# Softmax attention in a long single-core kernel: two fp32r score products on all 128 rows from stored high and low parts, and a differential unit that takes its second map whole before its first

## What is computed

```python
def diff_attention(q1, q2, k1, k2, v, lam):
    s1 = jnp.einsum('bqhd,bkhd->bhqk', q1, k1).astype(jnp.float32) * ATTN_SCALE
    s2 = jnp.einsum('bqhd,bkhd->bhqk', q2, k2).astype(jnp.float32) * ATTN_SCALE
    w = jax.nn.softmax(s1, axis=-1) - lam * jax.nn.softmax(s2, axis=-1)
    return jnp.einsum('bhqk,bkhe->bqhe', w, v.astype(jnp.float32))
...
def sink_attention(qg, k, v, sink, valid):
    s = jnp.einsum('bqhgd,bkhd->bhgqk', qg, k).astype(jnp.float32) * ATTN_SCALE
    ...
    p = jax.nn.softmax(jnp.concatenate([s, sink_col], axis=-1), axis=-1)[..., :-1]
    return jnp.einsum('bhgqk,bkhd->bqhgd', p, v.astype(jnp.float32))
```

## Time and profile before

| what | value |
|---|---|
| median of 3 runs | 3462.72 us (3462.21 to 3463.39) |
| span of the profiled execution | 3460.9 us, 1.8 below that median |
| mean granted TensorE clock | 0.962 |
| phase p0 beside the side job | 220 to 455 us |
| phase att: loads and context units | 459 to 504 us |
| phase att: 32 pairs | 504.8 to about 885 us |

### The profile page before, as it was taken

How to read it: one execution, slowest core, us unless ns; L and a number is a source line. 1 busy time by engine, 2 the same in 40 slices (tenths; PEclk the granted TensorE clock), 3 DMA queues, 4 the chain that set the end, 5 groups by cost and what they waited for, 6 DMA issues and landing times. The chain is left out here.

```text
span 3460.9 us, 51322 instructions
## 1 busy us (share of the span) xinstructions
PE 3176.7 (92%) x20902; PEld 2807.3 (81%) x20902; DVE 1711.3 (49%) x2697; ACT 1221.1 (35%) x2257; POOL 298.4 (9%) x357
## 2 busy tenths in 40 slices
PE   7999979999798999897999997979988999999988
PEld 4999967777587999775888976767856999999877
DVE  3459736666472211265526216746645445454343
ACT  4313235666562343124534114544423111111232
POOL 1000011100010000111211100002200000000010
PEclk9999999999899999998999998989999999999999
DMA  5556560000443221234211335110022111112332
GB/s 185 162 179 226 182 215 20 25 13 13 159 156 95 79 78 60 99 119 143 102 47 41 93 99 138 38 7 2 3 86 79 49 48 42 48 46 73 99 133 92
DMA packets 199262, 309.34 MB, mean 89 GB/s; under 512 B 43016, under 2 KB 133896, under 8 KB 197020
## 3 DMA queue, kind: packets, MB, share of 16 engines
q1 hardware_dynamic: 178448, 232.54, 21.1%
q0 software_dynamic: 20624, 74.13, 6.6%
HBM read 229.80 MB, written 76.81 MB: 89 GB/s over the span
## 5 line engine op out<-in xcount | busy, mean ns | idle before, releaser
L115 PE MATMUL p_pb<-p_w_hi,h_hi 128*128 128x416 f32 (+2 forms) x1168 | 408.2, 349 | 12.2 <-DVE p_w_lo L110 6.8
L116 PE MATMUL p_pb<-p_w_lo,h_hi 128*128 128x416 f32 (+2 forms) x1168 | 403.9, 346 | 0.0
L117 PE MATMUL p_pb<-p_w_hi,h_lo 128*128 128x416 f32 (+2 forms) x1168 | 403.8, 346 | 0.0
L115 PE MATMUL fu_pf<-h_hi,fu_w_hi 128*128 128x344 f32 (+1 forms) x1056 | 339.5, 322 | 8.7 <-DVE fu_pf L3747 8.7
L116 PE MATMUL fu_pf<-h_lo,fu_w_hi 128*128 128x344 f32 (+1 forms) x1056 | 340.5, 322 | 0.0
L117 PE MATMUL fu_pf<-h_hi,fu_w_lo 128*128 128x344 f32 (+1 forms) x1056 | 338.9, 321 | 0.0
L115 PEld LDWEIGHTS p_pb<-p_w_hi,h_hi 128*128 128x128 f32 x1168 | 221.0, 189 | 13.9 <-issue 12.6
L116 PEld LDWEIGHTS p_pb<-p_w_lo,h_hi 128*128 128x128 f32 x1168 | 220.7, 189 | 1.5
L117 PEld LDWEIGHTS p_pb<-p_w_hi,h_lo 128*128 128x128 f32 x1168 | 220.4, 189 | 1.3
L115 PEld LDWEIGHTS fu_pf<-h_hi,fu_w_hi 128*128 128x128 f32 x1056 | 199.9, 189 | 9.1 <-DVE fu_pf L3747 9.1
L117 PEld LDWEIGHTS fu_pf<-h_hi,fu_w_lo 128*128 128x128 f32 x1056 | 199.9, 189 | 0.0
(11 more groups left out here) (555 smaller groups left out, 6948.9 us busy)
## 6 DMA issues: line engine op xcount, KB each, us to landing
fu_raw<-in_ffn_up SPq DMA_DIRECT2D x88, 256.0 KB, 3.1
fd_raw<-in_ffn_down SPq DMA_DIRECT2D x44, 512.0 KB, 3.6
p_slab<-in_adaln_w SPq DMA_DIRECT2D x64, 256.0 KB, 3.3
la_qkv<-p SPq DMA_DIRECT2D x16, 1024.0 KB, 5.0
p<-p_o SPq DMA_DIRECT2D x60, 208.0 KB, 2.1
s_raw<-in_w_in POOLq DMA_DIRECT2D x48, 256.0 KB, 3.7
rT<-p_stage SPq DMA_DIRECT2D x10, 896.0 KB, 5.2
p_raw<-in_ab_w_in POOLq DMA_DIRECT2D x10, 832.0 KB, 7.2
```

The costliest lines, as they stand in the source:

```text
L115: pe.matmul(out, left[0], right[0], start=start, stop=False)
L116: pe.matmul(out, left[0], right[1], start=False, stop=False)
L117: return pe.matmul(out, left[1], right[0], start=False, stop=stop)
```

## The change

- The side job now stores two parts of each transposed block: a high part rounded to fp32r (ScalarE) and the rest (VectorE, `low_out`). The two A key heads are no longer doubled: 13 blocks, not 14. `rotated` is one buffer, not two, and the squares go to `tmp`.
- `rT` has the two parts as its first axis. Keys are loaded with their high part on partitions 0 to 63 and their low part on 64 to 127; a tile's queries are loaded with each part on both halves, into two buffers `Q` that are refilled tile by tile. Each load goes to 64 partitions, and SP issues them all.
- A score is now two fp32r products on all 128 rows (`whole`): the query's high part, then its low part, against the stacked keys.
- A `da` unit takes map 1 whole in part 0 and map 0 whole in part 1, and VectorE and ScalarE follow in that order. The waits change with it.

```diff
-                    sp.dma_start(rT[:, :, i * P:i * P + P].rearrange("c p t -> p c t"), stage[:, :, :]).then_inc(stage_out, 16)
+                    for part in range(2):
+                        sp.dma_start(rT[part, :, :, i * P:i * P + P].rearrange("c p t -> p c t"), stage[part][:, :, :].bitcast(F32)).then_inc(stage_out, 16)
...
-                    act.activation(stage[:, :, :], pt[:, 0:14, :], ACT.Copy).then_inc(evac, 1)
+                    act.activation(stage[0][:, :, :], pt[:, 0:QK_HEADS // 2, :], ACT.Copy).then_inc(staged, 1)
...
                         if i:
-                            dve.wait_ge(rotated, i)
+                            dve.wait_ge(turned, i)
...
+                def low_out(i):
+                    dve.wait_ge(staged, i + 1)
+                    lo_part(dve, stage[1][:, :, :], pt[:, 0:QK_HEADS // 2, :], stage[0][:, :, :]).then_inc(evac, 1)
...
-                sp.dma_start(KB[:, :, SEQ:], rT[KB_AT:KB_AT + 4, :, SEQ:].rearrange("c p t -> p c t")).then_inc(kb_ctx_in, 16)
...
+                def load_keys(keys, at, chunks, tokens, came):
+                    for part, half in enumerate(halves):
+                        sp.dma_start(keys[half, :, at:at + tokens.stop - tokens.start].bitcast(F32),
+                                     rT[part, chunks, :, tokens].rearrange("c (e d) t -> d (c e) t", d=HD)).then_inc(came, 16)
+
+                def load_queries(tile, first, chunk, came):
+                    for part in range(2):
+                        for half in halves:
+                            sp.dma_start(Q[ring[tile] % 2][half, first:first + 8, part, :].bitcast(F32),
+                                         rT[part, chunk:chunk + 4, :, P * tile:P * tile + P].rearrange("c (e d) t -> d (c e) t", d=HD)
+                                         ).then_inc(came[ring[tile] % 2], 16)
...
                 for tile in tiles_in_order:
+                    if ring[tile] + 2 < len(tiles_in_order):
+                        after = tiles_in_order[ring[tile] + 2]
+                        sp.wait_ge(scores, exps_before[last_of[tile] + 1])
+                        load_queries(after, A_HEADS, QB, qb_in)
+                        load_queries(after, 0, QA, qa_in)
...
-                pool.wait_ge(q1_in, 16)
+                pool.wait_ge(va_in, 16)
...
-                        for m in range(2):
-                            act.wait_ge(negmax, n + m + 1)
+                        for i, m in enumerate((1, 0)):
+                            act.wait_ge(negmax, n + i + 1)
...
-                        pe.wait_ge(expd, n - 1 if near_before else n)
+                        pe.wait_ge(expd, n - 2 if near_before and kind == "da" else n)
...
+                    def whole(out, head, keys, stop):
+                        queries = Q[ring[token_tile(u)] % 2]
+                        pe.matmul(out, queries[:, head, 0, :], keys, start=True, stop=False)
+                        return pe.matmul(out, queries[:, head, 1, :], keys, start=False, stop=stop)
+
                     if kind == "da":
-                        for c0, c1 in ((0, 512),) if part == 0 else ((512, 1024), (1024, ALLT)):
-                            for m, half in enumerate(halves):
-                                mm = pe.matmul(pS[m][:, c0:c1], qT[half, QB + j, q], KB[half, j, c0:c1], start=True, stop=True)
-                                if c1 == ALLT:
-                                    mm.then_inc(scores, 1)
+                        m = 1 - part
+                        for c0, c1 in ((0, 512), (512, 1024), (1024, ALLT)):
+                            mm = whole(pS[m][:, c0:c1], A_HEADS + 2 * j + m, KB[:, 2 * j + m, c0:c1], True)
+                        mm.then_inc(scores, 1)
...
                     if u < NU:
+                        n_tile = ring[token_tile(u)]
+                        pe.wait_ge((qb_in if units[u][0] in ("da", "dac") else qa_in)[n_tile % 2], 64 * (n_tile // 2 + 1))
```

More of the change, by code:

```diff
@@ L664, in project_even @@
         tmp = ph.sb("tmp", [P, QK_HEADS, HD])
-        rot = [ph.sb(f"rotated{s}", [P, 28, HD]) for s in range(2)]
+        rot = ph.sb("rotated", [P, QK_HEADS, HD])
         ss = ph.sb("ss", [P, QK_HEADS])
         rt = ph.sb("rt", [P, QK_HEADS])
-        stage = ph.sb("stage", [P, 14, P])
+        stage = ph.pair("stage", [P, QK_HEADS // 2, P])
         slab = [ph.sb(f"slab{s}", [P, MOD_BLK]) for s in range(2)]
@@ L852, in side @@
                         dve.wait_ge(spread, i + 1)
[L853 to L857, removed]
+                        dve.tensor_tensor(rot[:, :, :], rot[:, :, :], tmp[:, :, :], ALU.add).then_inc(rotated, 1)
+                        if i:
+                            low_out(i - 1)
+                    yield turn_at(n_all - 1) + 7
+                    low_out(n_all - 1)
+                def low_out(i):
+                    dve.wait_ge(staged, i + 1)
+                    lo_part(dve, stage[1][:, :, :], pt[:, 0:QK_HEADS // 2, :], stage[0][:, :, :]).then_inc(evac, 1)
                 def terms(i, k):
@@ L1268, in score @@
                         which = 0 if t == 0 else 2 if t == NT - 1 else 1
-                        left = [qT[half, QA + j, q] for half in halves]
-                        right = [KA[half, kv, :] for half in halves]
                         if part == 0:
                             for e in range(2):
-                                pe.matmul(pS[0][:, KEYS * e:KEYS * e + W3], left[e], right[e][:, near], start=True, stop=False)
-                            for e in range(2):
+                                whole(pS[0][:, KEYS * e:KEYS * e + W3], 2 * j + e, KA[:, kv, near], False)
                                 edges = pS[0][:, KEYS * e:KEYS * e + W3].rearrange("p (b k) -> p b k", b=3)[:, 0:3:2, :]
-                                mm = pe.matmul(edges, unit_r[:, :], mask[:, which, :, :], start=False, stop=True)
-                            mm.then_inc(banked, 1)
+                                pe.matmul(edges, unit_r[:, :], mask[:, which, :, :], start=False, stop=True)
                             return
-                        pe.matmul(pS[0][:, W3:512], left[0], right[0][:, far:far + P], start=True, stop=True)
-                        pe.matmul(pS[0][:, KEYS + W3:2 * KEYS], left[1], right[1][:, far:far + CTX], start=True, stop=True)
-                        pe.wait_ge(banked, sinks_before[u] - 3)
-                        pe.matmul(pS[0][:, 512:KEYS], left[0], right[0][:, far + P:far + CTX], start=True, stop=True).then_inc(scores, 2)
+                        whole(pS[0][:, W3:512], 2 * j, KA[:, kv, far:far + P], True)
+                        whole(pS[0][:, 512:KEYS], 2 * j, KA[:, kv, far + P:far + CTX], True)
+                        whole(pS[0][:, KEYS + W3:2 * KEYS], 2 * j + 1, KA[:, kv, far:far + CTX], True).then_inc(scores, 2)
                     elif part == 0:
```

88 lines of the change are left out of this document (41 added, 47 removed).

## The result

The changed kernel takes 3522.07 us (median of 4 runs, 3520.63 to 3524.55), the kernel before on the same chip 3463.05. The ratio is 1.0169, 95% interval [1.0155, 1.0184]: 59 us slower, where 40 were forecast. The time lies one microsecond inside the forecast's range of 3479 to 3523, and outside the 3489 to 3517 that had 0.6. Both costs of the forecast are there, and both are larger.

What follows compares the result with a forecast made beforehand. TensorE was taken as busy nearly all the time, with DMA to watch at the attention start. +22.6 + 1.5 + 17.6 - 1.1 = +40.6 on 3460.9 gave 3501.5, as median 3503 us; range 3479 to 3523.

Steps and rivals of the forecast that it cites:

- Both costs of the forecast: Late start of the attention phase, +22.6 us, and longer pairs, +17.6 us; forecast 3489 to 3517 us with chance 0.6.
- +22.6 us: Attention phase start: tile 0's B queries land at 527.4, where the first `da` unit started at 504.78.
- 11.8 MB at 210: Attention phase start: half-partition loads through tile 0's B queries, at 210 GB/s, take 56.2 us.
- 1.5 for the clock: First pair: TensorE starts at a lower clock after 20 us of standing, 1.5 us added.
- +17.6 us: The 32 pairs: 24 longer by 0.50 us and 8 with a press longer by 0.70.
- the last piece stays 4.26: Press pairs: transposes and value products with VectorE's row sum stay 4.26 us, so these pairs grow 0.70.
- a standing of 1.6 us should not lower the clock: Pairs: TensorE's wait of 1.60 us before the `wa` scores leaves its granted clock at 1.00.
- -1.1 us: p0 phase: 13 transposes instead of 14 in each of ten tiles save 1.1 us.
- Full-rate loads: Rival: attention phase loads run at full rate, start costs +2, rest as forecast; about 3481 us, chance 0.1.
- Gaps kept: Rival: TensorE's gaps between row shapes stay in the pairs, +37 there; +60 in all, 3523 us, chance 0.12.
- Both costs about half: Rival: queries land early through queue gaps and the pairs' wait is partly covered; 3475 to 3485 us, chance 0.1.
- The rival in which the window unit finds the second exponential done: Pairs: `wa` unit pays only its own work, 10.55 us a pair, -35 us, kernel near 3450; chance 0.05.

Runs made afterwards that it cites:

- experiment 1: Changed kernel, but ScalarE takes map 0's exponential first and the window scores wait for it alone: 3476.76 us, ratio 1.0044 to the kernel before.
- experiment 4: Kernel before the change, each key and query load cut into two of 64 partitions on the same queue: 3464.34 us, ratio 1.0003.
- experiment 6: Changed kernel with 128-partition loads from 192 DRAM rows per head: 3494.88 us; the faster one also takes map 0's exponential first: 3454.35 us.
- experiment 5: Kernel of experiment 1 with upper-half loads issued by POOL: 3487.68 us; with tile 0's queries ahead of A keys and values: 3479.94; both: 3482.26.

## Why the prediction was right, and where its sizes were off

**The direction and both mechanisms hold.** The wait on the second exponential was put at 1.60 us a pair; it measured 1.55, and taking it away (experiment 1) gave back 41.5 us over 31 intervals. The late start was put down to 64-partition loads at 210 GB/s and to doubled bytes; the windows show 205, experiment 4 shows that the rate is the partitions', and experiment 6 took 29 of the 33 us away.

**"+22.6 us" for the start: mis-sized, 32.7 measured from the start of the phase, and 4.0 more in the first pair.** The sum "11.8 MB at 210", values at 390 and nothing else comes to 15.5 MB at 236 GB/s on average. By the time the B queries are there, 16.3 MB have moved at 211:

```profile
457.50:534.60 77.10, 29.30 (x196) 27.27 (x194) 18.54 (x45) 21.00 (x78) 4.90 (x12) 0.70 1.10 211
458.00:473.00 15.00, 4.25 (x33) 4.05 (x32) 0.17 (x1) 0.00 (x0) 3.32 (x9) 0.73 1.10 187
519.00:523.00 4.00, 0.00 (x0) 0.00 (x0) 0.00 (x0) 0.00 (x0) 0.00 (x0) 0.50 1.04 375
525.00:529.00 4.00, 0.00 (x0) 0.00 (x0) 0.00 (x0) 0.00 (x0) 0.00 (x0) 0.50 1.20 167
```

As an estimate from these windows and the packets of the trace, three terms make most of the 10 us. Loads that the sum doesn't have were in flight beside the last queries, 0.4 MB of POOL's modulation sums and 0.3 MB of the next queries: 3.5 us. The B values' packets of 2,048 bytes took some 130 to 190 ns each while 64-partition loads were still in flight and 88 ns once they were alone (375 GB/s from 519 to 523), so these 2.6 MB took 9.2 us where 390 GB/s gives 6.7: 2.5. The first 15 us ran at 187 instead of 210: 1.6. The rest is 205 to 208 instead of 210 for the other halves, and less for short pieces, 167 from 525 to 529. No run takes these terms apart. The first pair, with 1.5 for the clock, also had the wait of 2.4 us for tile 0's A queries, which the sum did not have: it asked only when the B half lands.

**"+17.6 us" for the pairs: 24.7 measured.** Normal pairs were forecast 0.08 short (2 us in all), and three of them, ahead of the last three press pairs, are 12.6 (1 more). The press pairs carry the rest. Six of the eight are 13.79, 0.91 more than the 12.88 of before (one stood at 13.31), where "the last piece stays 4.26" gave 0.70: VectorE's maximum starts 0.37 us behind the transposes where it was 0.19, and the piece is 4.5. Two are 15.76 and 15.35. One of them, in windows:

```profile
750.00:752.00 2.00, 2.00 (x17) 1.61 (x17) 1.30 (x1) 0.60 (x1) 0.00 (x0) 1.00 0.04 10
752.00:754.00 2.00, 1.95 (x16) 1.67 (x14) 1.85 (x4) 1.30 (x4) 1.33 (x2) 1.00 0.00 0
754.00:756.00 2.00, 0.77 (x3) 0.67 (x4) 1.97 (x3) 0.73 (x3) 1.66 (x1) 1.00 0.00 0
756.00:758.00 2.00, 2.00 (x9) 1.89 (x8) 1.36 (x3) 0.10 (x1) 0.56 (x1) 0.51 0.39 156
```

TensorE was busy for 0.77 of 2 us, and then had a granted clock of 0.51, the lower of its two levels (1.2 GHz). The sentence "a standing of 1.6 us should not lower the clock" holds for the normal pairs, which stay at 1.00, and fails for these two. They are 1.6 and 2.0 us longer than the other six; in the longer one about 0.4 is a longer wait at the press, for with 128-partition loads (experiment 6, without the new order) the same pair is 14.19 and stays at 1.00. The other is 15.38 there, with the same dip, so the half-rate loads are not its cause. The second exponential is not needed either: experiment 6's faster kernel has one such pair, 14.49. All these dips follow a stand of 1.3 us at a press, but pair 20 of the changed kernel stands for 1.4 and keeps 1.00; what tells them apart is not shown.

**"-1.1 us" for p0: about -0.7.** The phase began at 454.2 to 458.4 us in six kernels with the same p0 code, but that scatter comes from ahead of p0, whose first product starts at 99.1 to 103.2. From that product to the start of the attention phase it is 355.1 to 356.1 us in these six, 355.4 on average, and 355.9 and 356.2 in the two with the p0 of before. A difference so near the scatter is only likely.

**The rivals.** Full-rate loads (3481): ruled out by the windows at 205 GB/s; where the rate was made full, the kernel gave 3495, since the pairs' loss stays and p0 is some 3 us longer. Gaps kept (3523, the nearest number): right in the sum by chance; maps take 1.17 us and window scores 1.64, so the gaps did go. Both costs about half (3475 to 3485): both were larger than forecast. The rival in which the window unit finds the second exponential done, 10.55 a pair: no run has it; even without that wait a pair is 11.03, because the first exponential and its 1.47 us still stand before the window scores.

## What to carry to other kernels

When a unit's sub-results are made in a new order, ask which of them frees the buffer that the next unit writes first, and give that one to the slow consumer first: here map 1 may be multiplied first, but map 0 must be exponentiated first. Before parts of an operand are stacked in partitions, look at what the loads become: 64 partitions halved the rate here (about 205 GB/s for 390), and an access pattern that begins with a 2 left two engines of sixteen (52 GB/s); rows laid out in DRAM in the order in which the partitions want them had neither cost (414 GB/s), for 3 us more of stores. Where a phase begins with more bytes than it can hide, their order moves the wait and not the end.

## What the runs showed of the hardware

- Loads to one half of the partitions move at about 205 GB/s at full share. Two queues with opposite halves, both in pieces of 4,096 bytes, moved 315 GB/s for 2 us (experiment 4); with POOL's pieces at 4,096 and SP's at 512 bytes it was 207 to 235 (experiment 5).
- Values that go to 128 partitions and stand in a queue behind halves flow slowly only while the halves are in flight: packets of 2,048 bytes took some 130 to 190 ns, then 88 ns, which is 391 GB/s from 520 to 522 in the changed kernel and 388 from 493 to 496 in experiment 4.
- Fp32r products on 128 rows beside each other, each with its weight load, start 0.23 us apart at 512 columns and 0.12 at 128. Idle times of 0.3 us, which stood before where TensorE went from a 64-row product to a 128-row one, are gone where all products have 128 rows.
- The same code up to p0 takes 99.1 to 103.5 us in the profiled runs, and single runs of the kernel before lie up to 10 us from their median (3454.9 beside 3464.8).
